# One share of dense tiles per pair of attention heads instead of two, in a two-layer transformer pair on one core

## The chip, the core and the metric

The kernel runs on one core of a Trainium2 chip. The metric is the device time of one execution in microseconds; the kernel before took 2789.5 us (median of 3 runs, 2788.83 to 2792.34). Of the core's engines the text names TensorE (PE, with PEld for its weight loads), VectorE (DVE), ScalarE (ACT), GpSimd (POOL) and SyncE (SP, which issues transfers).

## The reference

The input is a sequence of 512 rows of 1024 numbers, all in 32-bit floats. Two blocks of two layers each follow one another.

In a layer of the first block `h = x @ w_in` gives queries, keys and values of three attentions and three gates. The first ("fox") is causal softmax attention with a forgetting bias over 6 heads; the second is a stick-breaking attention over 5 heads; the third ("dsa") is softmax attention over 5 heads in which an index score picks at most 128 of the 512 keys per query. The outputs go through `w_up`, are multiplied with the sigmoids of the gates, summed, and projected by `w_out`; a layer norm and a feed-forward part follow.

In a layer of the second block a projection feeds a gated linear recurrence, a convolution branch and an attention ("nsa") of 8 heads with a compressed, a selected and a windowed branch. With 512 positions the selected and the windowed branch are both plain causal attention over all keys. The three results are concatenated and projected by `w_out`.

```
logits = q k^T * scale (+ bias);  w = softmax(mask(logits));  out = w v
merged = gate0 * (o_fox @ w_up_fox) + gate1 * (o_sb @ w_up_sb) + gate2 * (o_dsa @ w_up_dsa)
x = x + concat(y_nsa, y_lru, y_conv) @ w_out
```

## The kernel before, in words

Everything lies transposed (features on the partitions, 512 positions along the free axis). A dense product is cut into units of 8 tiles; a tile is one 128x128 piece of weights times 512 columns, and it takes three matmuls (`pe_tile`, L380 to L382), because weights and inputs are split into a high and a low part. The weights stream through four slots: SyncE loads `w_raw`, ScalarE rounds it to `w_hi` (L389), GpSimd makes `w_lo` (L404). When a unit is done, ScalarE takes its bank ("take", L1130 for the gates) and splits the weights of the slot's next unit.

Every engine has its own program, written out by hand; semaphores tie them. Nothing is reordered by a planner.

The softmax attentions fox, dsa and nsa share three functions, `pairs_pe`, `pairs_act` and `pairs_dve`. They run over "pairs": two heads (in dsa's last four pairs one head) at one block b of 128 queries, with (b + 1) * 128 keys; b runs 0, 1, 2, 3, 0, ... over the pairs n. A layer has 12 pairs in fox, 12 in dsa and 32 in nsa. For one pair:

- scores (TensorE, L494, and the mask L497) into the banks X[0] and X[1];
- the negated maximum (VectorE, L579);
- the exponential (ScalarE, L551) from these banks to the `work` tiles of the probabilities, with the row sums;
- the reciprocal and the scaling (VectorE, L587, L590 in nsa, L594), in place;
- the turn: transposes of the probabilities by TensorE (L507) into X[2] and ps[2];
- the copy of what was turned (ScalarE, L560);
- the values (TensorE, L521) into a bank that holds the output of two heads.

`depth` says how many buffers the probabilities and the turned copies have: 1 in fox, 2 in dsa and nsa. `exps(n)` waits for the turn of pair n - depth, and `copy(n)` for the values of pair n - depth. Scores of pair n wait until the exponentials of pair n - 1 have read the banks.

TensorE's order is in the loop of `pairs_pe`: scores of the next pair, `fill(n, 0)`, `turn(n)`, `fill(n, 1)`, `values(n - 1)`. Where scores need something of their own (`staged`: in fox at the first pair of each pair of heads, n + 1 = 4 and 8), they stand behind the turn. ScalarE's order is exps(n + 1), copy(n), and then takes and splits; in fox the takes stand in front of exps(n + 1), and a staging of the next queries and keys (`fox_stage`, L1172) follows copy(2) and copy(6). VectorE's is maximum(n + 1), scaling(n + 1), and then other work: in fox two rounds of a top-k search (L1317, L1319).

`fill` gives TensorE dense tiles that have nothing to do with the pair. In fox and dsa they are gate units (`gate_share`): `FOX_FILL` gives 3 units, 24 tiles, to each four pairs, so 3 tiles a call; `DSA_FILL` gives 2, 1 and 1 units, so 2, 1 and 1 tiles a call. In nsa they are tiles of the last projection (`out_fill`), one a call. ScalarE computes with `gate_ends` in which call a unit ends, and takes it one pair later (`round_gates`).

Of the kernel before, what the change touches and what calls it, by code (L numbers as in the profile page):

```python
# [28 lines left out]
QB = SEQ // P  # L29
# [28 lines left out]
FOX_FILL = ((4, 3), (7, 3), (10, 3))  # L58
STK_FILL = ((13, 3), (16, 2), (18, 2))
DSA_FILL = ((20, 2), (22, 1), (23, 1))  # L60
# [413 lines left out]
def half(e):  # L474
    return slice(64 * e, 64 * e + 64)


def count_before(pairs, n, e=0):

    return sum(len(h.heads) for h in pairs[:n]) + sum(x < e for x in pairs[n].heads)  # L480


def pairs_pe(S, pe, Z, h0, p0, pairs, ident, fill, ready, depth=2):
    nc = S.nc

    def scores(n):

        h = pairs[n]
        pe.wait_ge(Z.p, h0 + count_before(pairs, n))
        for sem, count in ready(n, "scores"):  # L490
            pe.wait_ge(sem, count)
        for e in h.heads:
            q, k = h.key(e)
            nc.tensor.matmul(S.X[e][:, 0:h.w], q, k, start=True, stop=False, skip_group_check=True)  # L494
        m, c = h.mask
        for e in h.heads:
            nc.tensor.matmul(S.X[e][:, c:h.w], S.idb[:, :], m, start=False, stop=True, skip_group_check=True).then_inc(Z.s, 1)  # L497

    def turn(n):
        h = pairs[n]  # L500
        pe.wait_ge(Z.ptc, h0 + count_before(pairs, n))
        for sem, count in ready(n, "turn"):
            pe.wait_ge(sem, count)
        for e in h.heads:
            pe.wait_ge(Z.scaled, h0 + count_before(pairs, n, e) + 1)
            for k in range(h.b + 1):
                m = nc.tensor.transpose((S.X[2], S.ps[2])[e][:, k * P:(k + 1) * P], h.probs[e][:, k * P:(k + 1) * P], ident)  # L507
            m.then_inc(Z.pt, 1)

    def values(n):  # L510
        h = pairs[n]
        pe.wait_ge(Z.ptc, h0 + count_before(pairs, n) + len(h.heads))
        for sem, count in ready(n, "values"):
            pe.wait_ge(sem, count)
        terms = [h.first] if h.first else []
        for k in range(h.b + 1):
            terms.append(lambda e, k=k: (h.value(e, k), h.turned[e][:, k * P:(k + 1) * P]))
        for x, term in enumerate(terms):
            for e in h.heads:
                v, p = term(e)  # L520
                m = nc.tensor.matmul(h.bank[half(e), h.b * P:h.w], v, p, start=(h.begins and x == 0),  # L521
                                     stop=(h.ends and x == len(terms) - 1), skip_group_check=True)
        m.then_inc(Z.o, 1)

    N = len(pairs)
    scores(0)
    for n in range(N):
        staged = n + 1 < N and any(True for _ in ready(n + 1, "scores"))
        if n + 1 < N and not staged:
            scores(n + 1)  # L530
        fill(n, 0)
        turn(n)
        if staged:
            scores(n + 1)
        fill(n, 1)
        if n >= 1:
            values(n - 1)
    values(N - 1)
# [66 lines left out]
def fox_pairs(S):  # L605

    pairs = []
    for n in range(3 * QB):
        i, b = divmod(n, QB)
        w = (b + 1) * P  # L610
        pairs.append(Pair(S, n, b, lambda e, b=b, w=w: (S.wk[e][:, b * P:w], S.wk[2 + e][:, 0:w]), (S.causb[:, :], b * P),
                          lambda e, k, i=i: vt_head(S, k, V_FOX, 2 * i + e), (S.ps[3], S.X[3])[i % 2], depth=1))
    return pairs
# [15 lines left out]
def dsa_pairs(S):  # L629

    pairs = []
    keys = [tile_rows(S, u, e) for e, u in ((0, A_DKIK), (1, A_S4KDK))]
    for n in range(3 * QB):
        i, b = divmod(n, QB)
        w = (b + 1) * P
        m0 = (b * (b + 1) // 2 - 1) * P
        q = [tile_rows(S, A_DQ + i if i < 2 else A_S4D4Q, e) for e in range(2)]
        pairs.append(Pair(S, n, b, lambda e, b=b, w=w, q=q: (q[e][:, b * P:w], keys[e][:, 0:w]),
                          (S.dmask[:, m0:m0 + w], 0) if b else (S.chunkb[:, :], 0),
                          lambda e, k: vt_head(S, k, V_DSA, 0), (S.ps[3], S.X[3])[i % 2], (0, 1) if i < 2 else (1,)))  # L640
    return pairs
# [302 lines left out]
def gate_fill(S, pe, L, i, first, tiles):  # L944


    for x in tiles:
        j, k = divmod(x, KT)
        u = A_GATE + first + j
        s = u % SLOTS  # L950
        if k == 0:
            pe.wait_ge(S.lo_ready[s], GA(L, u, i) + 1)
            pe.wait_ge(S.bank_free[(u - 2) % SLOTS], GA(L, u - 2, i) + 2)
        pe_tile(S, s, k, S.ps[u % 2][:, :], S.xh, S.xl, k, k == 0, k == KT - 1)
        if k == KT - 1:
            S.last.then_inc(S.unit_done[s], 1)


def gate_share(S, pe, L, fill, c, calls):

    first, units = fill
    n = units * KT
    gate_fill(S, pe, L, 0, first, range(n * c // calls, n * (c + 1) // calls))


def gate_ends(fill, calls):

    n = fill[1] * KT
    return [next(c for c in range(calls) if n * (c + 1) // calls >= KT * (j + 1)) for j in range(fill[1])]
# [5 lines left out]
def a_tensor(S, pe):  # L975
    nc = S.nc
    ident = S.con[:, C_ID:C_ID + P]
    for L in range(DEPTH):
# [11 lines left out]
        for v in range(A_NVT):  # L990
            if v >= 2:
                pe.wait_ge(S.vt_done, L * A_NVT + v - 1)
            for t in range(QB):
                m = nc.tensor.transpose(S.X[2 + v % 2][:, t * P:(t + 1) * P],
                                        S.qkv[:, A_VT[v] * SEQ + t * P:A_VT[v] * SEQ + (t + 1) * P], ident)
# [24 lines left out]
        def fox_ready(n, what):  # L1020
# [3 lines left out]
            if what == "values" and n == 2 * QB:  # L1024
                return [(S.fox.out, L * 3 + 1)]
            return []

        pairs_pe(S, pe, S.fox, L * 24, L * 12, fox_pairs(S), ident,
                 lambda n, x: gate_share(S, pe, L, FOX_FILL[n // QB], 2 * (n % QB) + x, 8), fox_ready)

        pe.wait_ge(S.fox.out, L * 3 + 2)
        for i in range(2):
# [7 lines left out]
        def dsa_ready(n, what):  # L1040
# [4 lines left out]
            if what == "values" and n == 2 * QB:  # L1045
                return [(S.dsa.out, L * 3 + 1)]
            return []

        pe.wait_ge(S.mask_ready, L + 1)
        pairs_pe(S, pe, S.dsa, L * 20, L * 12, dsa_pairs(S), ident,  # L1050
                 lambda n, x: gate_share(S, pe, L, DSA_FILL[n // QB], 2 * (n % QB) + x, 8), dsa_ready)

        for i in range(2):
            for jj in range(4):
# [15 lines left out]
                for w, x, stop in ((S.wh, S.rh, False), (S.wh, S.rl, False), (S.wl, S.rh, True)):  # L1070
                    for e, out in enumerate((XS, XD)):
                        m = nc.tensor.matmul(out, w[s][half(e), 5 * P:6 * P], x[half(e), 5 * SEQ:6 * SEQ], start=False, stop=stop)
# [50 lines left out]
def a_scalar(S, act, T):  # L1123
# [12 lines left out]
    for L in range(DEPTH):  # L1136
# [19 lines left out]
        def gate_take(j):  # L1156
            u = A_GATE + j
            take(u, G(u), cols(S.gates, j), ACT.Copy, 2)

        def gate_takes(fill, calls, c):  # L1160

            for j, end in enumerate(gate_ends(fill, calls)):
                if end == c:
                    gate_take(fill[0] + j)
# [21 lines left out]
        def round_gates(fill, n):  # L1186

            if n == 0:
                return
            i, m = divmod(n - 1, QB)  # L1190
            for x in range(2):
                gate_takes(fill[i], 2 * QB, 2 * m + x)

        def fox_after(n):
            if n % QB == 2 and n < 2 * QB:
# [25 lines left out]
        with act.Fori(0, 2) as i:  # L1221
            for jj in range(4):
                for d in range(3):
                    t = cols(S.gates, i * SLOTS + d * KT + jj)
                    m = nc.scalar.activation(t, t, ACT.Tanh, scale=0.5)
# [312 lines left out]
def GB(L, u, i=0):  # L1538

    return DEPTH * A_GROUPS + L * B_GROUPS + u // SLOTS + i  # L1540


def BF(L, u, i=0):

    s = u % SLOTS
    mine = [v for v in B_BANKED if v % SLOTS == s]
    return 1 + DEPTH * A_GROUPS + L * len(mine) + sum(v < u for v in mine) + i


def seq(t, j):  # L1550
    return t[:, j * SEQ:(j + 1) * SEQ]
# [73 lines left out]
def out_fill(S, pe, L, i, n):  # L1625


    j, k = divmod(n, KT)
    o, kk = divmod(k, 4)
    g = GB(L, B_OUTL, i)  # L1630
    if n == 0:
        if i == 0:
            pe.wait_ge(S.lru_done, L + 1)
        else:
            pe.wait_ge(S.mc_ready, L * 4 + 5)
    if k == 0:
        pe.wait_ge(S.lo_ready[j], g + 1)
        pe.wait_ge(S.first_added, L * 8 + i * 4 + j + 1)
    if k == 4:
        pe.wait_ge(S.bank_free[(j - 1) % SLOTS], BF(L, B_OUTL + j - 1, i) + 1 if j else BF(L, B_OUTL + 3, i))  # L1640
    pe_tile(S, j, k, S.ps[o][:, :], S.xh, S.xl, i * 4 + kk, kk == 0, kk == 3)
    if k == 3:
        S.last.then_inc(S.first_out, 1)
    if k == KT - 1:
        S.last.then_inc(S.unit_done[j], 1)
# [20 lines left out]
def b_tensor(S, pe):  # L1666
# [4 lines left out]
    for L in range(DEPTH):  # L1671
# [64 lines left out]
        for t in range(4):  # L1736
            m = nc.tensor.matmul(S.ps[1][:, :], S.ones[:, :], seq(S.cacc, t), start=(t == 0), stop=(t == 3))
# [24 lines left out]
        for q in range(4):  # L1762
            if q == 2:
                for t in range(4):
                    pe.wait_ge(S.cl_sq, L * 4 + t + 1)
                    m = nc.tensor.matmul(S.X[1][:, :], S.ones[:, :], S.lnsq[t][:, :], start=(t == 0), stop=(t == 3))
# [57 lines left out]
        def nsa_ready(n, what):  # L1824
# [3 lines left out]
            if what == "values" and n % (2 * QB) == 0 and n >= 4 * QB:  # L1828
                return [(S.mn_y, L * 4 + n // (2 * QB) - 1)]
            return []  # L1830

        pairs_pe(S, pe, S.nsa, L * 64, L * 32, nsa_pairs(S), ident,
                 lambda n, x: out_fill(S, pe, L, n // 16, n % 16 * 2 + x), nsa_ready)

        pe.wait_ge(S.first_added, L * 8 + 9)
        for j in range(4):
# [470 lines left out]
def program(nc, T, out):  # L2307
    with ExitStack() as ctx:
# [17 lines left out]
        @block.tensor  # L2326
        def _(pe):
            a_tensor(S, pe)
            b_tensor(S, pe)
# [174 lines left out]
```

## Time and profile before

| | |
|---|---|
| median of 3 runs | 2789.5 us |
| profiled execution | 2787.53 us, its span 2785.7 us |
| TensorE busy | 2693.0 us (97%) |
| VectorE, ScalarE, GpSimd busy | 1432.0, 1143.5, 1062.1 us |
| fox of the first layer, scores to last values | about 213 to 301 us into the span |
| dsa of the first layer | about 396 to 446 us |
| nsa of the two layers | about 2211 to 2339 and 2619 to 2747 us |

A line of the timeline gives the start of a group of equal instructions in us from the start of the span, the time from there to the end of the last, the engine and line, what it writes and reads, and how many there are. In brackets stand the idle time of the engine before it and what ended it. A record of a short matmul lasts 0.27 us though the next one starts after 0.11, because matmuls are pipelined.

### The profile page before, as it was taken

The numbers are of one execution on the slowest core, as the hardware profiler recorded it, in microseconds if no ns is written. First come the engines' busy times: TensorE is split into PE (matmuls) and PEld (weight loads), VectorE is DVE, ScalarE is ACT, GpSimd is POOL, SyncE is SP. The second block draws the span as 40 slices with busy tenths as digits, with TensorE's granted clock in tenths as the row PEclk, the third lists the DMA queues.
The fourth block names the chain that finished last, engine by engine and source line by source line (L and its number), as shares of the span: only waits on it lengthen the run. The fifth ranks groups of instructions, "written<-read, shape, count | busy, mean of one in ns | idle before, by whom it ended". The sixth has DMA issues, their size and how long they took to land.

```text
span 2785.7 us, 36067 instructions
## 1 busy us (share of the span) xinstructions
PE 2693.0 (97%) x12740; PEld 2046.6 (73%) x12740; DVE 1432.0 (51%) x2446; ACT 1143.5 (41%) x1982; POOL 1062.1 (38%) x430
## 2 busy tenths in 40 slices
PE   8999999999999989999999999999999999999998
PEld 6866666788888778576666888886687767787766
DVE  2067646562223220776474633232688764688764
ACT  2334435252223342444452522233436654337554
POOL 4422212344444434222123444443247522347612
PEclk9999999999999999999999999999999999999999
DMA  4221111222332223111122322322223211223211
GB/s 166 90 68 46 53 38 61 83 83 91 104 98 98 83 68 105 54 54 46 38 68 76 100 97 98 98 90 83 68 96 114 85 39 54 78 96 121 76 39 54
DMA packets 61316, 220.24 MB, mean 79 GB/s; under 512 B 6928, under 2 KB 7056, under 8 KB 61200
## 3 DMA queue, kind: packets, MB, share of 16 engines
q1 hardware_dynamic: 60624, 217.12, 23.8%
q8 instruction: 73, 1.20, 0.2%
q10 hardware_dynamic: 576, 1.57, 0.2%
q14 instruction: 43, 0.35, 0.0%
HBM read 216.57 MB, written 2.10 MB: 78 GB/s over the span
## 4 chain that ended last, share of the span: by engine, by line
PE 89%; DVE 5%; ACT 2%; DVEq 1%; POOL 1%; issue 1%; DMA 0%; ACTq 0%; SPq 0%
PE bank L380 24%; PE bank L382 24%; PE bank L381 24%; PE bank L494 3%; PE bank L521 3%; PE bank L507 2%; PE bank L843 1%; PE bank L709 1%; PE bank L497 1%; POOL w_lo L404 1%; PE bank L1014 1%; PE bank L731 1%; PE bank L727 1%; PE bank L701 1%; DVE proj L1376 1%
## 5 line engine op out<-in xcount | busy, mean ns | idle before, releaser
L404 POOL TENSOR_TENSOR w_lo<-w_raw,w_hi 128x1024 fp32r<-128x1024 f32 x404 | 1011.5, 2512 | 1694.1 <-ACT w_hi L389 1687.8
L380 PE MATMUL bank<-x_hi,w_hi 128*128 128x512 f32 x2128 | 883.0, 415 | 30.4 <-DVE x_lo L2301 11.0
L382 PE MATMUL bank<-x_hi,w_lo 128*128 128x512 f32 x2128 | 837.0, 393 | 0.0
L381 PE MATMUL bank<-x_lo,w_hi 128*128 128x512 f32 x2128 | 836.7, 393 | 0.0
L389 ACT ACTIVATE w_hi<-w_raw 128x1024 fp32r<-128x1024 f32 x400 | 419.6, 1055 | 435.1 <-PE bank L382 376.4
L380 PEld LDWEIGHTS bank<-x_hi,w_hi 128*128 128x128 f32 x2128 | 404.1, 190 | 149.9 <-issue 51.7
L382 PEld LDWEIGHTS bank<-x_hi,w_lo 128*128 128x128 f32 x2128 | 403.5, 190 | 87.4
L381 PEld LDWEIGHTS bank<-x_lo,w_hi 128*128 128x128 f32 x2128 | 404.7, 190 | 81.6 <-issue 9.6
L380 PE MATMUL bank<-rhs_hi,w_hi 128*128 128x512 f32 x624 | 245.4, 393 | 6.4 <-DVE rhs_lo L1449 6.4
L381 PE MATMUL bank<-rhs_lo,w_hi 128*128 128x512 f32 x624 | 243.5, 390 | 0.0
L382 PE MATMUL bank<-rhs_hi,w_lo 128*128 128x512 f32 x624 | 243.2, 390 | 0.0
L551 ACT ACTIVATE work<-bank,neg_max 128x128 f32<-128x128 f32 (+3 forms) x216 | 112.0, 523 | 213.8 <-DVE neg_max L579 162.4
L1514 DVE TENSOR_TENSOR ffn_sum<-ffn_sum,bank 128x512 f32 x64 | 43.9, 688 | 286.1 <-PE bank L382 286.1
L2071 DVE SCALAR_TENSOR_TENSOR bank<-glu_out,params_b_cur,bank 128x512 f32<-128x512 f32 x216 | 152.7, 752 | 34.2 <-issue 34.2
L1504 DVE TENSOR_TENSOR work<-work 128x512 f32<-128x512 f32 x64 | 90.8, 1419 | 139.1 <-ACT rhs_hi L1271 139.1
L1361 DVE TENSOR_SCALAR proj<-proj 128x1024 f32<-128x1024 f32 (+2 forms) x8 | 9.3, 1227 | 267.7 <-ACT proj L1130 267.7
L380 PEld LDWEIGHTS bank<-rhs_hi,w_hi 128*128 128x128 f32 x624 | 117.5, 188 | 36.3 <-issue 11.7
L382 PEld LDWEIGHTS bank<-rhs_hi,w_lo 128*128 128x128 f32 x624 | 117.5, 188 | 24.7
L381 PEld LDWEIGHTS bank<-rhs_lo,w_hi 128*128 128x128 f32 x624 | 117.6, 188 | 23.8
L579 DVE TENSOR_REDUCE neg_max<-bank 128x1 f32<-128x128 f32 (+3 forms) x216 | 96.1, 485 | 65.7 <-PE bank L497 64.2
L1269 ACT ACTIVATE work<-bank 128x512 f32<-128x512 f32 x64 | 38.0, 594 | 193.2 <-PE bank L382 185.0
L1130 ACT ACTIVATE proj<-bank 128x512 f32 (+1 forms) x52 | 31.0, 596 | 201.5 <-PE bank L382 201.5
(390 smaller groups left out, 3327.5 us busy)
## 6 DMA issues: line engine op xcount, KB each, us to landing
w_raw<-w SPq DMA_DIRECT2D x404, 512.0 KB, 3.4
ln_in<-x SPq DMA_DIRECT2D x4, 512.0 KB, 7.7
out<-residual SPq DMA_DIRECT2D x8, 256.0 KB, 2.2
p_raw<-p ACTq DMA_DIRECT2D x2, 512.0 KB, 4.1
constants<-con SPq DMA_DIRECT2D x1, 455.0 KB, 10.4
cos<-cos SPq DMA_DIRECT2D x1, 256.0 KB, 10.5
sin<-sin SPq DMA_DIRECT2D x1, 256.0 KB, 10.2
params_b<-prm_b ACTq DMA_DIRECT2D x1, 256.0 KB, 3.1
```

Source lines behind the costliest of these rows:

```text
L380: nc.tensor.matmul(out, wh, xh, start=first, stop=False)
L381: nc.tensor.matmul(out, wh, xl, start=False, stop=False)
L382: S.last = nc.tensor.matmul(out, wl, xh, start=False, stop=last)
L389: S.nc.scalar.activation(S.wh[s][:, :], S.raw[s][:, :], ACT.Copy).then_inc(S.hi_ready[s], 1)
L404: S.nc.gpsimd.tensor_tensor(S.wl[s][:, :], S.raw[s][:, :], S.wh[s][:, :].bitcast(F32), ALU.subtract).then_inc(S.lo_ready[s], 1)
L494: nc.tensor.matmul(S.X[e][:, 0:h.w], q, k, start=True, stop=False, skip_group_check=True)
L507: m = nc.tensor.transpose((S.X[2], S.ps[2])[e][:, k * P:(k + 1) * P], h.probs[e][:, k * P:(k + 1) * P], ident)
L521: m = nc.tensor.matmul(h.bank[half(e), h.b * P:h.w], v, p, start=(h.begins and x == 0), stop=(h.ends and x == len(terms) - 1), skip_group_ ...
L551: nc.scalar.activation(h.probs[e][:, 0:h.w], S.X[e][:, 0:h.w], ACT.Exp, bias=S.nm[x][:, :], accum_out=S.rs2[:, x:x + 1]).then_inc(Z.p, 1)
L579: nc.vector.tensor_reduce(S.nm[2 * h.par + e][:, :], S.X[e][:, 0:h.w], AX, ALU.max, negate=True).then_inc(Z.max, 1)
L1504: nc.vector.tensor_tensor(h, S.wk[j % 2][:, :], S.wk[j % 2][:, :], ALU.mult)
L2071: stt(out=S.X[t % 2][:, :], in0=S.uc[:, bass.ds(i * 3 + (k + t * UC_W), SEQ)], scalar=S.curB[:, bass.ds(i * 3 + (k + PB_DW + t * CONV_K), ...
```

## The change

`fill` is called once per pair, ahead of the turn, and gives what the two calls gave together. In fox and dsa it asks for one of 4 shares in place of two of 8; in nsa it issues the two tiles one behind the other. ScalarE's list of takes is computed for 4 calls.

```diff
@@ pairs_pe
         if n + 1 < N and not staged:
             scores(n + 1)
-        fill(n, 0)
+        fill(n)
         turn(n)
         if staged:
             scores(n + 1)
-        fill(n, 1)
         if n >= 1:
             values(n - 1)
@@ a_tensor (fox; dsa alike, with DSA_FILL)
-                 lambda n, x: gate_share(S, pe, L, FOX_FILL[n // QB], 2 * (n % QB) + x, 8), fox_ready)
+                 lambda n: gate_share(S, pe, L, FOX_FILL[n // QB], n % QB, QB), fox_ready)
@@ a_scalar, round_gates
-            for x in range(2):
-                gate_takes(fill[i], 2 * QB, 2 * m + x)
+            gate_takes(fill[i], QB, m)
@@ b_tensor (nsa)
-                 lambda n, x: out_fill(S, pe, L, n // 16, n % 16 * 2 + x), nsa_ready)
+                 lambda n: [out_fill(S, pe, L, n // 16, n % 16 * 2 + x) for x in range(2)], nsa_ready)
```

## Rows read from the trace of the kernel before

**Rows 1.** The page, busy us (share of the span) and instructions.

```profile
PE 2693.0 (97%) x12740; PEld 2046.6 (73%) x12740; DVE 1432.0 (51%) x2446; ACT 1143.5 (41%) x1982; POOL 1062.1 (38%) x430
```

**Rows 2.** The waits of TensorE: total us, times, longest.

```profile
PE bank L494 <- ACT work L551: 9.6, 6, 2.2
...
PE bank L507 <- DVE work L594: 4.0, 6, 0.8
```

**Rows 3.** Timeline, fox of layer 1, turn of pair 5 to scores of pair 7.

```profile
254.75 0.60 PE L507 MATMUL bank<-constants,work 128*128 128x128 f32 x4
255.11 0.48 PE L380 MATMUL bank<-x_hi,w_hi 128*128 128x512 f32 x1
...
257.36 0.44 PE L521 MATMUL bank<-work,v_tok 128*64 128x128 f32 x4
257.73 1.98 PE L494 MATMUL bank<-work,work 128*128 128x512 f32 x4
...
255.45 0.58 ACT L551 ACTIVATE work<-bank,neg_max 128x384 f32<-128x384 f32 x1 [3.72 <-PE bank L507]
...
256.48 0.20 ACT L551 ACTIVATION_READ_ACCUMULATOR work<-bank,neg_max 128x1 f32 x1
```

**Rows 4.** Timeline, fox of layer 1, exponentials of pair 5 and values of pair 3.

```profile
248.72 0.48 ACT L551 ACTIVATE work<-bank,neg_max 128x256 f32<-128x256 f32 x1 [1.53 <-DVE neg_max L579]
...
249.54 0.20 ACT L551 ACTIVATION_READ_ACCUMULATOR work<-bank,neg_max 128x1 f32 x1
...
250.08 1.09 PE L521 MATMUL bank<-work,v_tok 128*64 128x128 f32 x16
```

**Rows 5.** Timeline, fox of layer 1, around the staged scores of pair 4.

```profile
236.23 0.20 ACT L551 ACTIVATION_READ_ACCUMULATOR work<-bank,neg_max 128x1 f32 x1
...
238.42 2.32 ACT L1172 ACTIVATE work<-proj 64x512 f32<-64x512 f32 x4
...
239.67 1.04 PE L507 MATMUL bank<-constants,work 128*128 128x128 f32 x8
240.84 0.68 PE L494 MATMUL bank<-work,work 128*128 128x128 f32 x4
...
241.98 0.49 DVE L579 TENSOR_REDUCE neg_max<-bank 128x1 f32<-128x128 f32 x2
...
242.30 0.37 ACT L551 ACTIVATE work<-bank,neg_max 128x128 f32<-128x128 f32 x1
...
242.91 0.20 ACT L551 ACTIVATION_READ_ACCUMULATOR work<-bank,neg_max 128x1 f32 x1
...
243.68 0.88 PE L521 MATMUL bank<-work,v_tok 128*64 128x128 f32 x12
```

**Rows 6.** Timeline, end of dsa of layer 1 and start of the products behind it.

```profile
443.80 0.60 ACT L560 ACTIVATE work<-bank 128x512 f32<-128x512 f32 x1 [1.75 <-PE bank L507]
...
444.50 0.60 ACT L1130 ACTIVATE gates<-bank 128x512 f32<-128x512 f32 x1
...
449.17 0.77 PE L380 MATMUL bank<-rhs_hi,w_hi 128*128 128x512 f32 x1 [3.04 <-DVE rhs_lo L1449]
```

**Rows 7.** Timeline, nsa of layer 1: its start, and a later pair.

```profile
2217.53 0.66 PE L507 MATMUL bank<-constants,work 128*128 128x128 f32 x2 [0.82 <-DVE work L594]
...
2218.43 0.20 ACT L551 ACTIVATION_READ_ACCUMULATOR work<-bank,neg_max 128x1 f32 x1
...
2219.41 1.23 PE L494 MATMUL bank<-b_ks,b_q 64*128 64x256 f32 x4
...
2259.88 0.58 ACT L551 ACTIVATE work<-bank,neg_max 128x384 f32<-128x384 f32 x1 [2.28 <-DVE neg_max L579]
...
2260.92 0.20 ACT L551 ACTIVATION_READ_ACCUMULATOR work<-bank,neg_max 128x1 f32 x1
...
2261.53 0.92 PE L494 MATMUL bank<-b_kw,b_q 64*128 64x384 f32 x4
```

**Rows 8.** Stretch of dsa: its length, busy us by engine, PEclk, DMA.

```profile
395.00:446.00 51.00, 49.83 (x311) 33.69 (x309) 20.27 (x55) 24.32 (x69) 9.41 (x4) 1.00 0.13 42
```

More of the change, by code:

```diff
@@ L1050, in a_tensor @@
         pairs_pe(S, pe, S.dsa, L * 20, L * 12, dsa_pairs(S), ident,
-                 lambda n, x: gate_share(S, pe, L, DSA_FILL[n // QB], 2 * (n % QB) + x, 8), dsa_ready)
+                 lambda n: gate_share(S, pe, L, DSA_FILL[n // QB], n % QB, QB), dsa_ready)
         for i in range(2):
```

## The prediction, made before the change was run

> **What bounds the kernel now.** I read the busy table first: TensorE works 2693 of 2785.7 us [rows 1]. The profiled execution took 2787.53 us, so 1.8 us lie around its span, and the median of the runs shown, 2789.5, is 2.0 above it. TensorE is the bound nearly everywhere, so the change can gain only what TensorE waits for in the three attentions, or what it pays for going from one kind of matmul to another. The waits of TensorE come next: its scores waited 9.6 us in all for exponentials and its turns 4.0 us for the scaled probabilities [rows 2]. Those 4.0 us are the whole stock of waits that a later turn can remove. Then I read the timelines of the stages, TensorE beside ScalarE, for who ends each wait and how much room there is where none is seen.
>
> Names: pair n has scores S(n), exponentials E(n), turns T(n), copies C(n) and values V(n). fox is the first attention, dsa the second, nsa the third; they have 12, 12 and 32 pairs in each of two layers, 112 in all. A share is 9 dense matmuls in fox, 6 or 3 in dsa, 3 in nsa.
>
> **What moves.** Before, TensorE runs S(n+1), share, T(n), share, V(n-1), S(n+2). After, it runs S(n+1), both shares, T(n), V(n-1), S(n+2). No matmul is added or dropped. ScalarE's takes of finished gate units stay at the same pairs, since with 24, 16 or 8 tiles the last tile of a unit falls in the same pair for 8 calls as for 4; no DMA is issued elsewhere. Nor does V(n-1) get a new wait: it needs C(n-1), for which T(n) has waited already. What is late next is S(n+2). It needs E(n+1), because scores write over the banks that the exponentials read. In dsa and nsa E(n+1) needs only its own maximum and a much older turn (depth 2). In fox (depth 1) it writes over the probabilities that T(n) reads, so E(n+1) starts when T(n) is over. Between T(n) and S(n+2) there were a share and V(n-1), now V(n-1) alone.
>
> **Transitions.** Per pair the path from the last transpose to V was 255.08 to 257.36, 2.28 us [rows 3]: 255.08 is the group's start 255.11 minus 0.03, or 254.75 plus three steps of 0.11. Of it 9 matmuls at 0.229 are 2.06, which are merely moved. What remains, 0.22, is to be set against the new step from a transpose straight to V. From V to S the same rows give it: the last V starts at 257.53 (start plus 0.44 minus the last one's 0.27), S at 257.73, 0.20 later, that is one 128-column pass (0.11) and 0.10 of emptying. I take 0.21, since T to V changes the shape of the array's use (128x128 to 128x64) as V to S does. Gain 0.01 x 112, nothing. Bounds: 0.03, as a dense matmul's record stands behind the last transpose [rows 3], and 0.40, as S stands behind T at the start of a head pair [rows 5]; that is -0.19 to +0.18 each, -21 to +20 us over 112 pairs.
>
> The trace's 0.10 agrees with a rule of the Trainium skill (TensorEngine Tiling, "Key Properties"): a change of tiling mode, as opposed to tile, drains the engine. By it T to V costs a drain just as share to V did, so this item is nothing; without it the item would be -11 us (112 x 0.10).
>
> **fox, the cost.** In the trace T(5) starts its last transpose at 255.08 and E(6) starts at 255.45, released by the turn: 0.37 later. E(6) is over at 256.68 and S(7) comes at 257.73 [rows 3]: 1.05 of room, which a share of 2.06 had made. From E's end to a waiting S I take 0.05 (an estimate: nothing lies between but the signal, and if it is 0.2 the sum grows by 2). E takes 1.02 for 256 columns [rows 4] and 1.23 for 384 [rows 3], so 0.21 a step, 0.81 for 128 [rows 5] and 1.44 for 512. From V to S is V's record less 0.27 plus the 0.20: 0.37 for one block (257.36 to 257.73), 0.81 for three [rows 5], 1.02 for four [rows 4], 0.59 for two by the same steps. After the change S(n+2) stands ready at 0.21 + V(n-1) behind the last transpose, and its banks at 0.42 + E(n+1). The new wait is the difference, 0.21 + E(n+1) - V(n-1):
> - S(3), S(7), S(11): E of 384, V of one block: 0.21 + 1.23 - 0.37 = 1.07 each, 3.2 together.
> - S(6), S(10): E of 256, V of four blocks: 0.21 + 1.02 - 1.02 = 0.2 each, 0.4. In the trace E(5) was released by VectorE's maximum [rows 4]; with the turn 2.06 later it is the turn.
> - S(2): no values yet, and scores may follow a transpose at 0.11: 0.42 + 1.02 - 0.11 = 1.3.
> - S(4), S(8) are issued behind T(3), T(7) (staged), so S(5), S(9) come close behind them. Set the last transpose of T(2) to 0. E(3) ends at 0.37 + 1.44 = 1.81. In the trace VectorE reduces S(4) at 241.98, 5.55 after E(3)'s end 236.43, with its top-k rounds before [rows 5]; after: 7.36. E(4) starts 0.32 later and takes 0.81, so S(5) may go at 8.54. TensorE: V(1) at 0.21, 0.59 long, 18 matmuls 4.21 (18 x 0.229 and 0.09 at their start), T(3) to its last transpose 0.77, then 0.11: S(4) at 5.9. S lasts 0.68 - 0.27 + 0.11 = 0.52 [rows 5], mask to V 0.21 (two of 0.055 and the 0.10), V(2) 0.81, ready at 7.4. Wait 1.1. Against it S(4) loses a wait of 0.29: it started 0.40 behind the last transpose (239.67 + 0.77), because ScalarE's staging ended at 240.74 [rows 5]. Net 0.8 each, 1.6.
> - S(1), V(11): as before; the latter waits for a copy that starts behind V(10).
>
> Sum 3.2 + 0.4 + 1.3 + 1.6 = 6.5 a layer, 13.1 for two. Nothing later gives it back, as TensorE is the bound behind it.
>
> **dsa.** The periods between scores stay, and E doesn't wait for the turn. But the last turn T(11) is 0.69 later (3 x 0.229), and C(11) started on it, with ScalarE idle 1.75 before. Behind C(11) on ScalarE are the take of the last gate unit, a split and the rounding of the outputs, and for those TensorE waits 3.04 [rows 6]. The take started at 444.50; it will follow C(11), which starts at 443.80 + 0.69 and lasts 0.60: 445.09 at the latest, +0.59. I take +0.5 a layer, as records of neighbours overlap a little, +1.0. Bounds: 0 if the delay is hidden, 1.4 with the full 0.69.
>
> **nsa.** In steady state nothing: S(n+2) follows S(n+1) at the same distance and the least room in front of it, 0.41, hangs on maxima and not on turns [rows 7]. Copies are up to 0.69 later, but ScalarE idled longer than that before E, 2.28 at that pair [rows 7]. At the start T(0) waited 0.8 for scaled probabilities [rows 7, 2]; the second share now lies in that wait. S(2) stood at 2219.41 and is then held by E(1), over at 2218.63, so 2218.68: -0.7 a layer, -1.4. The other waits of this kind (1.2 us at pair 5) are refunded to nobody, since E(6) holds S(7) there; lower end -4.0 for all of rows 2.
>
> **Sum.** 13.1 + 1.0 - 1.4 + 0 = +12.7 us on the profiled 2787.5: 2800.2; on the median of 2789.5, 2802. That is 0.45%.
>
> **Rivals.**
> 1. The turn hands over to the values for less than I say. At 0.11 (no emptying) the item is -11 and the time 2791, no change; at 0.03 it is -20, and the time 2782, faster. It decides against me from 0.10 less a pair. For it: the record of a dense matmul 0.03 behind a transpose. Against: the 0.20 from V to S, and that the dense record behind the transpose lasts 0.48, so that its start is no start of streaming. 7% for no change, 4% for faster.
> 2. VectorE becomes fox's bound. Its top-k rounds fill most of the 5.55 us quoted above, and E(4) had no slack. If some four maxima a layer come late by 1.2 each: +9.6, 2812. For it: VectorE's 5.55 against a pair of 7.3 us (V(3) at 250.08, V(4) at 257.36, [rows 3, 4]). Against: the turn that releases E is later too. 7%.
> 3. The waits drop TensorE's clock in fox. Each new gap is 1.3 at most, and the dsa stage has TensorE idle for 1.17 us (51.00 less 49.83), nearly all of it in one wait before S(1), at a granted clock of 1.00 [rows 8]. At half the clock the 216 matmuls of fox's shares alone would take 0.2 more each, +43 a layer. 2%: over 2830.
> 4. fox does not pay: exponentials are early enough by some path that I overlooked. The room of 1.05 against the 2.06 that is removed speaks against it, as does the releaser in the row. The time is then 2789. 4%.
>
> **Numbers.** Mine 76%, rival 1 11%, rival 2 7%, rival 3 2%, rival 4 4%. What a measurement tells from no change is about 0.2%, 5.6 us: faster 0.05, same 0.11, slower 0.84. Range 2793 to 2812: down by half of my fox waits and a part of rival 1, up to rival 2 or a T to V of 0.29.
>
> **What would show it.** In fox of the changed kernel: a wait of S on E in the list of waits, six to eight times a layer, most near 1 us, about 14 us more than the 9.6 of now; E released by the turn at every pair; from the last transpose to V about 0.21. In dsa the wait of 3.04 becomes about 3.5. In nsa the first turn's wait is gone, S(2) is some 0.7 nearer to S(0), and the stage is otherwise as long as before. I am wrong if fox's stage is less than 3 us a layer longer, or if nsa gets shorter by more than 2.

## The result, and the profile after

| | median, us | runs | ratio to before, 95% interval |
|---|---|---|---|
| before | 2791.4 | 8 | |
| after | 2802.2 | 8 | 1.0042 [1.0029, 1.0054] |

The change makes the kernel slower by 0.42%, 8 to 15 us by the interval. The profiled execution of after took 2806.32 us (span 2804.5), 18.8 more than that of before. Not all of that comes from the changed code: the matmuls of code that is the same in both already differ in where the clock is low (below), and TensorE's wait for its first inputs, within the first 60 us, was 12.6 us here and 11.0 in before (10.8 to 13.3 over the profiles of all kernels). So the steps are judged on the stages alone, and the total on the medians.

The waits of TensorE, as in [rows 2] (lines from L532 on have moved by one or two):

```profile
PE bank L494 <- ACT work L550: 24.2, 22, 2.2
...
PE bank L380 <- DVE rhs_lo L1447: 6.8, 2, 3.4
```

Scores wait 24.2 us for exponentials where they waited 9.6 [rows 2]: 14.6 more, in 16 more places. Of these 12.8 are fox's, in six places a layer (2 x (1.17 + 3 x 1.01 + 2 x 1.10)); the other 1.8, in four places, are nsa's. The row of turns that wait for scaled probabilities (4.0) is gone.

The timeline of fox of layer 1 around T(5), which [rows 3] show before:

```profile
262.32 0.60 PE L507 MATMUL bank<-constants,work 128*128 128x128 f32 x4
262.84 0.44 PE L521 MATMUL bank<-work,v_tok 128*64 128x128 f32 x4
...
264.30 1.98 PE L494 MATMUL bank<-work,work 128*128 128x512 f32 x4 [1.01 <-ACT work L550]
...
263.01 0.58 ACT L550 ACTIVATE work<-bank,neg_max 128x384 f32<-128x384 f32 x1 [5.98 <-PE bank L507]
...
264.04 0.20 ACT L550 ACTIVATION_READ_ACCUMULATOR work<-bank,neg_max 128x1 f32 x1
```

These five lines show how the loss comes about. The exponentials start 0.36 behind the last transpose (262.32 + 3 x 0.11 = 262.65), as before; they are over at 264.24, 1.23 later. But now only V(4), four matmuls, stands between the turn and the next scores, and the scores wait. The 1.01 in brackets is the idle time behind the last record of V; scores can start 0.07 ahead of that record's end (the 0.27 of a record less the 0.20 from V to S), so the whole wait is 1.08. From the last transpose to V is 0.19.

Exponentials of 256 columns, which VectorE released before [rows 4], are now released by the turn, and the first ones of a head pair still by the maximum:

```profile
255.55 0.47 ACT L550 ACTIVATE work<-bank,neg_max 128x256 f32<-128x256 f32 x1 [3.38 <-PE bank L507]
...
249.82 1.13 PE L494 MATMUL bank<-work,work 128*128 128x256 f32 x4 [1.10 <-ACT work L550]
...
248.96 0.37 ACT L550 ACTIVATE work<-bank,neg_max 128x128 f32<-128x128 f32 x1 [1.35 <-DVE neg_max L578]
```

The end of dsa, as in [rows 6]:

```profile
452.82 0.60 ACT L559 ACTIVATE work<-bank 128x512 f32<-128x512 f32 x1 [2.11 <-PE bank L507]
...
453.31 0.59 ACT L1129 ACTIVATE gates<-bank 128x512 f32<-128x512 f32 x1
...
457.98 0.47 PE L380 MATMUL bank<-rhs_hi,w_hi 128*128 128x512 f32 x1 [3.42 <-DVE rhs_lo L1447]
```

The start of nsa, as in [rows 7]: the turn waits for nothing, and S(2) for E(1).

```profile
2237.91 0.63 PE L507 MATMUL bank<-constants,work 128*128 128x128 f32 x2
2238.80 1.22 PE L494 MATMUL bank<-b_ks,b_q 64*128 64x256 f32 x4 [0.26 <-ACT work L550]
```

The steps from one S to the next (start to start of L494 in the timeline, us) show which pair pays. fox, S(2) to S(3) and so on to S(11), layer 1; "idle" is that in front of the later one:

| | S3 | S4 | S5 | S6 | S7 | S8 | S9 | S10 | S11 | sum |
|---|---|---|---|---|---|---|---|---|---|---|
| before | 6.50 | 10.84 | 3.65 | 6.62 | 6.62 | 10.84 | 3.65 | 6.62 | 6.62 | 61.96 |
| after | 7.67 | 12.58 | 2.63 | 6.80 | 7.68 | 12.58 | 2.62 | 6.82 | 7.67 | 67.05 |
| idle, after | 1.01 | 0 | 1.10 | 0.15 | 1.01 | 0 | 1.10 | 0.15 | 1.01 | 5.5 |

From S(2) to S(11) it is 5.09 more; layer 2 agrees (67.02 against 61.96). In front of S(2) TensorE is idle for 1.17, and 0.16 more are lost to the record's length (0.27 less the 0.11 after which scores may follow a transpose): 1.33. fox costs 6.4 a layer, 12.8 in all.

The step S(1) to S(2) itself grew by 2.72, from 7.09 to 9.81. Of that 1.33 are the ones just named; the other 1.4 are not the change. Behind the 2.2 us for which TensorE waits before S(1), in both kernels, its granted clock is at the half level (1.2 of 2.4 GHz) for a while: dense matmuls last 0.63 and come every 0.43, then 0.39 and every 0.23. The mean granted clock was 0.67 from 217.00 to 226.90 in after, and 0.76 from 216.50 to 223.50 in before. How long the half level lasts differs from execution to execution of the same instructions (table below, "S1 to S2"), with this change and without it; the same holds at the start of nsa.

### The profile page after: what moved, and what is told of

Read it like the earlier page. It is cut to its first block, busy times and chain, and to the rows that moved or that the text cites. A ratio compares the mean times of both kernels' runs of the same rounds, so it can differ in the third digit from the quotient of the medians.

```text
span 2804.5 us, 36067 instructions
## 1 busy us (share of the span) xinstructions
PE 2698.7 (96%) x12740; PEld 2063.5 (74%) x12740; DVE 1429.5 (51%) x2446; ACT 1145.5 (41%) x1982; POOL 1061.1 (38%) x430
## 4 chain that ended last, share of the span: by engine, by line
PE 88%; DVE 6%; ACT 3%; DVEq 1%; issue 1%; POOL 1%; DMA 0%; ACTq 0%; SPq 0%
PE bank L380 24%; PE bank L381 23%; PE bank L382 23%; PE bank L494 3%; PE bank L521 3%; PE bank L507 2%; PE bank L842 1%; PE bank L1013 1%; ACT work L550 1%; PE bank L708 1%; POOL w_lo L404 1%; PE bank L497 1%; PE bank L730 1%; PE bank L726 1%; PE bank L700 1%
## 5 line engine op out<-in xcount | busy, mean ns | idle before, releaser
L404 POOL TENSOR_TENSOR w_lo<-w_raw,w_hi 128x1024 fp32r<-128x1024 f32 x404 | 1010.5, 2510 | 1713.9 <-ACT w_hi L389 1707.3
L380 PE MATMUL bank<-x_hi,w_hi 128*128 128x512 f32 x2128 | 875.1, 411 | 31.5 <-DVE x_lo L2299 12.6
L380 PEld LDWEIGHTS bank<-rhs_hi,w_hi 128*128 128x128 f32 x624 | 117.8, 189 | 37.1 <-issue 12.4
```

The source lines that it names most:

```text
L380: nc.tensor.matmul(out, wh, xh, start=first, stop=False)
L404: S.nc.gpsimd.tensor_tensor(S.wl[s][:, :], S.raw[s][:, :], S.wh[s][:, :].bitcast(F32), ALU.subtract).then_inc(S.lo_ready[s], 1)
```

## The experiments

Kernels of one table stand beside runs of the kernel before on their chip. `tail` is dense work that `pairs_pe` issues behind the turn and behind staged scores, and `fox_tiles(n, a, b)` issues the tiles from a up to b, b left out, of the six of pair n:

```diff
 def pairs_pe(..., fill, ready, tail=lambda n: None):
         if staged:
             scores(n + 1)
+        tail(n)
         if n >= 1:
             values(n - 1)
```

| kernel | fox, tiles ahead + behind the turn | dsa, nsa: shares | median, us (before) | ratio, 95% interval | S2 to S11, us | S1 to S2, both layers | TensorE's scores on exponentials |
|---|---|---|---|---|---|---|---|
| after | 6 + 0 | 1, 1 | 2802.2 (2791.4) | 1.0042 [1.0029, 1.0054] | 67.05 | 9.81, 9.55 | 24.2 |
| fox alone | 6 + 0 | 2, 2 | 2801.0 (2790.6) | 1.0037 [1.0024, 1.0051] | 67.04 | 9.80, 8.45 | 22.4 |
| fox apart | 3 + 3 | 1, 1 | 2788.6 (2790.6) | 0.9992 [0.9981, 1.0003] | 61.96 | 8.41, 8.10 | 12.0 |
| second buffers | 6 + 0 | 1, 1 | 2788.3 (2790.6) | 0.9990 [0.9980, 0.9999] | 61.69 | 8.10, 8.11 | 13.2 |
| 5 and 1 | 5 + 1 | 1, 1 | 2791.4 (2790.6) | 1.0000 [0.9991, 1.0009] | 63.21 | 8.64, 7.72 | 15.7 |
| 4 and 2 | 4 + 2 | 1, 1 | 2787.1 (2791.6) | 0.9983 [0.9974, 0.9992] | 61.28 | 7.10, 8.12 | 11.8 |
| 0 and 6 | 0 + 6 | 1, 1 | 2801.9 (2791.6) | 1.0043 [1.0030, 1.0056] | 67.53 | 7.08, 6.99 | 12.0 |
| no top-k | 6 + 0 | 1, 1 | 2800.7, one run | | 65.56 | 8.39, 8.39 | 21.9 |
| nsa's first pair | 6 + 0 | 1, 1 at pair 0 | 2802.7, one run | | 67.06 | 6.82, 9.71 | 23.4 |
| the gains | 4 + 2 | 2, 1 | 2787.4 (2790.6) | 0.9983 [0.9975, 0.9992] | 61.30 | 8.39, 7.13 | 11.8 |
| before, second buffers | 3 + 3 | 2, 2 | 2790.3 (2790.6) | 0.9996 [0.9988, 1.0005] | 61.95 | 8.48, 8.21 | 9.6 |

S2 to S11 is layer 1's, from the start of S(2) to that of S(11); before it is 61.96, and S1 to S2 is 7.09 and 7.13. The last column, in us over both layers, holds 4.4 us in front of S(1) of fox in every kernel; the rest of before's 9.6 are 2.3 in front of S(1) of dsa and 2.8 in nsa.

**Fox alone, and fox apart.** One edit on after each:

```diff
@@ fox alone: dsa with two shares again (nsa alike, with out_fill)
-                 lambda n: gate_share(S, pe, L, DSA_FILL[n // QB], n % QB, QB), dsa_ready)
+                 lambda n: gate_share(S, pe, L, DSA_FILL[n // QB], 2 * (n % QB), 8), dsa_ready,
+                 lambda n: gate_share(S, pe, L, DSA_FILL[n // QB], 2 * (n % QB) + 1, 8))
@@ fox apart: fox with 3 tiles ahead of the turn and 3 behind it
-                 lambda n: gate_share(S, pe, L, FOX_FILL[n // QB], n % QB, QB), fox_ready)
+                 lambda n: fox_tiles(n, 0, 3), fox_ready, lambda n: fox_tiles(n, 3, 6))
```

> fox has one share per pair, dsa and nsa have two as before. My theory (the loss is fox's exponentials, which are released by the turn): fox costs what it costs in the changed kernel, +15 us on the profiled execution of before (13 by the forecast, 15 by the stage in the changed kernel's trace), a ratio of 1.0047 to 1.0055; waits of scores on exponentials 24 us, 22 times, as in the changed kernel. Rival 'every pair pays, in all three attentions' (the step from a turn to values): 112 pairs share the loss, 24 of them are here, so fox alone costs 3 us, ratio 1.001. Where mine holds, this kernel is 1 to 2 us slower than the changed kernel, because nsa's gain of 2.7 and dsa's loss of 0.5 are left out.

> dsa and nsa have one share per pair, fox has two again (3 tiles ahead of the turn, 3 behind it). My theory: the whole loss is fox's, so this is 2 us faster than before (nsa -2.7, dsa +0.5 or +1 in its end), ratio 0.9992, no wait of scores on exponentials beyond the 9.6 us of before. Rival 'every pair pays': 88 of 112 pairs still have one share, so 0.8 of the loss stays, ratio 1.003.

Fox alone shows all of the loss (1.0037; 112 pairs sharing it would have given 1.001), and fox apart none of it. The loss is fox's. My ratio for fox alone, 1.0047 to 1.0055, was too high: its upper part came from the 15 us of the profiled stage, part of which is the clock's, and the 12.8 of the steps are 1.0046, inside the measured interval. I had also expected it to be 1 to 2 us slower than after, as it lacks nsa's gain; the medians (2801.0 and 2802.2) don't resolve that. Its scores wait 22.4 us in 18 places, not 24 in 22, as the four places of nsa are gone. The waits on exponentials in fox apart are 12.0, not the 9.6 that I expected: in nsa scores now wait a little where the turn did before. That is no extra time, since the same kernel's turns lost 2.7 of their 4.0.

**Second buffers** for fox's probabilities, place and number of the shares as in after (odd pairs get two tiles of their own; shortened):

```diff
@@ Pair of fox
+                          probs=(otok(S, 6), otok(S, 7)) if n % 2 else None))
@@ pairs_act, exps
-            if n >= depth:
-                act.wait_ge(Z.pt, h0 + count_before(pairs, n - depth) + len(pairs[n - depth].heads))
+            if n >= 2:
+                act.wait_ge(Z.pt, h0 + count_before(pairs, n - 2) + len(pairs[n - 2].heads))
```

> The changed kernel with a second pair of buffers for fox's probabilities (two tiles of the outputs' buffer that are free in that stage): exponentials of pair n+1 now need the turn of pair n-1 and not of n. The turned copy keeps one buffer. Nothing else differs; order and place of the shares are those of the changed kernel. My theory: the waits before S(2), S(3), S(6), S(7), S(10), S(11) go, because exponentials start on their maximum, some 2 us sooner. S(5) and S(9) keep about 0.7 (the maximum of the staged S(4) and the exponentials of 128 columns, 2.3 us, against mask and V(2), 1.5 us behind its start). fox is then within 1 us a layer of before, total between -2 and +1 against before, ratio 0.9993 to 1.0003. Rival VectorE (its two top-k rounds a pair set when maxima and scalings come): a second buffer does not hasten VectorE, most of the 14.6 us of waits stay, now released by the maximum, ratio 1.004. Rival 'merged shares themselves cost' (more steps between kinds of matmul or the clock): ratio 1.004 with no waits in the list.

The waits of fox that are left behind S(1), in layer 1, are these two:

```profile
246.09 1.13 PE L495 MATMUL bank<-work,work 128*128 128x256 f32 x4 [0.36 <-ACT work L551]
...
273.70 1.13 PE L495 MATMUL bank<-work,work 128*128 128x256 f32 x4 [0.36 <-ACT work L551]
```

The six others are gone, fox is as short as before (61.69 against 61.96), and with it the loss: 0.9990, a little below the 0.9993 to 1.0003 that I expected. So what cost time was that E(n+1) must follow T(n), which rests on one buffer, and not the shares as such. VectorE's part in it is measured below. S(5) and S(9) kept 0.36, half of the 0.7 I expected: from the start of S(4) to the end of its exponentials is 1.83 (244.21 to 246.04), where I had put 2.3.

**Before with second buffers** is the control: the same two edits on the kernel before.

> The kernel before with the second pair of buffers for fox's probabilities, as a control for the kernel that has them and one share. Theory: with a share of 2.06 us behind the turn no score waits for exponentials, so earlier exponentials are worth nothing: ratio 0.9995 to 1.0005, steps S to S of fox from S(2) on equal to before within 0.1 but for S(4) and S(8), which wait 0.13 for the staging. Rival: the second buffers are a gain of their own (ScalarE or VectorE ahead), ratio 0.998, and the level time of the kernel with one share and second buffers was two effects that cancel.

0.9996: alone they are worth nothing, as their exponentials were early already. What they gave above is the cure of the change's own wait.

**5 and 1, 4 and 2** tiles: `fox_tiles(n, 0, 5)` and `(n, 5, 6)`, or 4 in place of 5.

> The changed kernel, in fox 5 of a pair's 6 tiles ahead of the turn and 1 behind it (behind staged scores too). One tile is 0.69 us. My theory, by the subtraction it rests on: the wait is 1.07 - 0.69 = 0.4 before S(3), S(7), S(11); nothing before S(6), S(10); 1.1 - 0.69 = 0.4 before S(5), S(9); 1.2 - 0.69 = 0.5 before S(2). Together 2.5 a layer where the changed kernel has 7.3, so 9.6 us fewer waits in two layers, and fox is some 5 us (2 layers) longer than before: about +3 on before with nsa's and dsa's parts, ratio 1.001. Rival VectorE: waits before S(5), S(9) stay 1.1. Rival T to V: the step from a turn to values is gone, for it is a dense tile again, so all of the loss goes at once: as the kernel with 3 and 3 tiles.

> The changed kernel, in fox 4 of a pair's 6 tiles ahead of the turn and 2 (1.37 us) behind it. Theory (a wait is what is left of 0.21 + E - V after the dense tiles between turn and scores): 1.37 is more than the largest wait of the changed kernel, 1.17, so every wait of scores on exponentials behind S(1) is gone; fox from S(2) on is as long as with 3 and 3 tiles; total 2 us under before, ratio 0.9992, the same as 3 and 3 within the measurement. Rival 'the loss grows with each tile that is moved': a third of it stays, ratio 1.001.

The waits of 5 and 1 (timeline, layer 1; S(2), S(3), S(5), and S(7), S(9) repeat the last two):

```profile
224.17 1.56 PE L494 MATMUL bank<-work,work 128*128 128x384 f32 x4 [0.47 <-ACT work L551]
231.16 1.98 PE L494 MATMUL bank<-work,work 128*128 128x512 f32 x4 [0.31 <-ACT work L551]
...
245.70 1.13 PE L494 MATMUL bank<-work,work 128*128 128x256 f32 x4 [0.39 <-ACT work L551]
```

One tile behind the turn takes 0.70 off each of 1.17, 1.01 and 1.10, and three matmuls at 0.229 are 0.69. fox is then 1.9 longer a layer than before, where I had put 2.5, and the time is level with before (1.0000, expected 1.001). With two tiles behind it no wait is left but the one before S(1), as I expected. I had also expected fox to be level with before, and it is 0.68 a layer shorter (61.28 against 61.96, in both layers). The fourth tile ahead of T(3) and T(7) gives the staging 0.69 more time, and S(4) and S(8), which stood 0.40 behind the last transpose [rows 5], now follow it 0.11 later (241.02 to 241.13 in its timeline): two of 0.29, most of the 0.68. So a wait is a plain difference of two paths, the third tile behind the turn buys nothing, and ahead of it it buys something.

**0 and 6**: one share, all behind the turn (`fox_tiles(n, 0, 0)` and `(n, 0, 6)`).

> The changed kernel, in fox all 6 tiles of a pair behind the turn: one share per pair, as in the changed kernel, but in the other place. Theory (place and not number of the shares sets the loss): no wait of scores on exponentials; a turn now follows the scores directly and could wait for its scaled probabilities, but the exponentials start 4 us sooner, so it does not, but for T(0), within 1.5 us a layer. fox within 1.5 us a layer of 3 and 3 tiles, ratio 0.9990 to 1.0003. Rival 'one share of six tiles costs, wherever it stands': ratio 1.004. Rival 'the turn waits instead' (scaled probabilities late at every pair by 0.5 or more): 12 us over both layers, ratio 1.004, with the waits put down to the scaling.

My theory failed here: 1.0043, as slow as after, by other waits. The rival that one share costs wherever it stands gave this ratio too, but second buffers have one share and no loss, and the waits say what it was. In front of T(3) and S(4) (layer 1; TensorE, then ScalarE):

```profile
236.16 0.66 PE L521 MATMUL bank<-work,v_tok 128*64 128x128 f32 x8
237.84 1.09 PE L507 MATMUL bank<-constants,work 128*128 128x128 f32 x8 [1.03 <-ACT work L560]
240.09 1.19 PE L494 MATMUL bank<-work,work 128*128 128x128 f32 x4 [1.15 <-issue]
```

```profile
236.92 0.87 ACT L560 ACTIVATE work<-bank 128x384 f32<-128x384 f32 x2 [3.26 <-PE bank L521]
237.68 2.31 ACT L1175 ACTIVATE work<-proj 64x512 f32<-64x512 f32 x4
```

With one buffer of turned probabilities C(2) needs V(1), and T(3) needs C(2), which empties its banks. A share used to lie between V(1) and T(3). Where the scores are staged nothing is between them now: T(3) waits 1.03 for the copy, and S(4) 1.15, by its place for the staging that stands behind the copy on ScalarE (it ends at 239.99, and S(4) starts at 240.09; the row itself names no releaser). T(7), S(8) and T(11) do the same: 5.4 a layer. Behind the two waits in front of S(4) the granted clock falls to the half level as well, in both layers, but not at S(8), where they are as long:

```profile
232.00:240.00 8.00, 5.91 (x36) 4.42 (x34) 5.95 (x16) 4.51 (x11) 2.10 (x1) 0.99 0.18 66
240.00:243.20 3.20, 3.11 (x11) 2.69 (x12) 1.02 (x4) 2.33 (x6) 1.57 (x1) 0.50 0.00 0
243.20:260.00 16.80, 16.73 (x97) 12.82 (x95) 12.82 (x33) 5.11 (x14) 3.20 (x2) 1.00 0.19 63
```

(Stretch, its length, busy us of PE, PEld, DVE, ACT, POOL, granted clock, DMA.) The half clock costs 1.5 there: S(4) to S(5) is 7.21, S(8) to S(9) 5.71. So the rule "behind the turn is safe" would be as false as "ahead of it": each place has a buffer of depth 1 behind it, the probabilities the one and the turned copy the other, and the share has to be cut so that both are covered.

**No top-k**, for VectorE's part. It leaves out the two rounds in each pair of fox, and so computes another result; it is one run, and only its waits are read:

```diff
@@ fox_after
-            for x in range(2):
-                top_round(S, dve, x)
```

> The changed kernel without the two top-k rounds that VectorE has in each pair of fox (24 of 32 selection rounds are left out; the key selection of the third attention is another one). It asks what part VectorE has in the waits. Theory: only S(5) and S(9) wait for VectorE: in the changed kernel its rounds hold the maximum of S(4) until 1.44 us behind the scores' start (247.19 to 248.64), in the kernel with double buffers it comes at 0.70. So these two waits fall from 1.10 to 0.36, and those before S(2), S(3), S(6), S(7), S(10), S(11) stay at 1.17, 1.01, 0.15, 1.01, 0.15, 1.01. Waits of fox fall from 6.7 to 5.2 a layer. Rival VectorE (it bounds fox): all waits fall below 0.4.

```profile
250.35 1.13 PE L494 MATMUL bank<-work,work 128*128 128x256 f32 x4 [0.36 <-ACT work L550]
...
264.83 1.98 PE L494 MATMUL bank<-work,work 128*128 128x512 f32 x4 [1.01 <-ACT work L550]
```

S(5) (and S(9)) went from 1.10 to 0.36, and the rest stayed at 1.17, 1.02, 0.15, 1.01, 0.15, 1.01. VectorE holds 0.74 in two places a layer, 3 us in all. In after one sees it hold the maximum of S(4), whose last product starts at 247.52 (247.19 plus three steps of 0.11):

```profile
247.88 0.68 DVE L1317 MATCH_REPLACE8 idx_score<-top,idx_score 128x512 f32<-128x512 f32 x1
248.63 0.49 DVE L578 TENSOR_REDUCE neg_max<-bank 128x1 f32<-128x128 f32 x2
```

**Nsa's first pair**: one share at pair 0, two at all others; one run, read for its steps.

```diff
-                 lambda n: [out_fill(S, pe, L, n // 16, n % 16 * 2 + x) for x in range(2)], nsa_ready)
+                 lambda n: [out_fill(S, pe, L, n // 16, n % 16 * 2 + x) for x in range(1 if n else 2)], nsa_ready,
+                 lambda n: n and out_fill(S, pe, L, n // 16, n % 16 * 2 + 1))
```

> The changed kernel, in nsa only the first pair with both tiles ahead of the turn, all others with one ahead and one behind as before. It asks which pair gives nsa's gain. Theory: the step S(1) to S(2) stays 5.03 (0.7 under before), for the second tile fills the wait of T(0); the step S(5) to S(6) goes back from 4.44 to 5.34, because the tile ahead of T(4) and what stands behind it on ScalarE and GpSimd are again where they were. Steady steps 0.01 longer each. Rival: the step of pair 5 depends on the start alone (GpSimd's products shifted against VectorE), and stays 4.44.

S(1) to S(2) stayed at 5.01, S(5) to S(6) went back to 5.34, and steady steps are 0.01 longer, as expected. So nsa's gain has two places: 0.7 comes from the share of pair 0, and 0.9, in front of S(6), from the shares of the pairs behind it; the turn that had waited there is that of pair 4.

**The gains** alone: fox 4 and 2, dsa two shares, nsa one.

> The parts of the change that gain, without those that lose: nsa with both tiles ahead of the turn, dsa with two shares, fox with 4 tiles ahead of the turn and 2 behind it. Theory: nsa gives 1.6 a layer (0.7 before S(2), 0.9 before S(6)) less nothing, fox is level with before from S(2) on, dsa too, with the wait in front of the products behind it back at 3.04: 3 us under before, ratio 0.9989. It differs from the kernel with 4 and 2 tiles in fox by dsa's second share alone, 0.5 a layer at most, so the two can't be told apart by time. Rival: the gain of nsa is given back later (a wait of the products behind it grows by as much), ratio 1.0000.

0.9983, and the wait in front of the products behind dsa is back at 3.0 (6.4 in two layers, against 6.8). By its steps it gains 5 us and not the 3 that I expected, since fox of 4 and 2 tiles is not level but 1.4 shorter over both layers; the times don't tell the two apart (0.9989 lies inside the interval). This and the kernel with 4 and 2 tiles beat both before and after; their two medians, 2787.4 and 2787.1, are alike.

## Why the prediction was right

I forecast +12.7 us, 2802; the median is 2802.2. By step:

- **Transitions** (nothing, bounds -21 to +20): right. T to V takes 0.19 where I took 0.21. In nsa the 25 steps from S(6) to S(31) are 0.15 shorter together, in dsa S(2) to S(11) 0.1 of 37.1, so that is a gain of 0.01 a pair. The drain that the Trainium skill (TensorEngine Tiling, "Key Properties") names for a change of mode is paid on either path: 0.19 from T to V and 0.20 from V to S, where one pass is 0.11.
- **fox, S(3), S(7), S(11)**: 1.07 forecast, 1.08 measured. **S(6), S(10)**: 0.2 and 0.22 (0.15 of idle time and the 0.07). **S(2)**: 1.3 and 1.33. **S(5), S(9)**: 1.1 and 1.17, of which the refund at S(4), S(8) leaves 0.72 for both steps together (0.8 forecast). Sum 6.5 forecast, 6.4 measured. The mechanism was tried from three sides: more dense work between turn and scores shortens each wait by its own length, a second buffer removes them, undoing fox removes the loss.
- **dsa**: +0.5 a layer forecast for the wait in front of the products. The wait grew by 0.38 (3.04 to 3.42), and the way from S(11) to the products by 0.47 (10.49 to 10.96); the steps give back 0.1. That is +0.4 a layer, 0.7 in all.
- **nsa**: -0.7 a layer at S(2), measured -0.74 (5.77 to 5.03). Wrong was the next sentence: the waits of turns behind it (1.2 us) "are refunded to nobody". They are those of T(4), not of pair 5 as I wrote, and the scores behind them are S(6), which E(5) holds. S(5) to S(6) is 0.90 shorter, in both layers. I had looked only at whether E holds the next scores, and it does, for 0.59 us. But E came sooner, since its maximum did. The size of the error is 1.8 us of 2790, below what the times can tell; the trace shows it. With it nsa is 1.8 shorter a layer, 3.6 in all, where -1.4 in all was forecast: taken over both layers, my own sign of being wrong ("shorter by more than 2") came up for this stage.
- **Rivals.** The cheap step from turn to values is out by the 0.19, and by fox apart, whose 88 merged pairs are no slower and no faster than the parts of nsa and dsa explain (-2.9 us by the steps, 0.9990; 0.9992 measured). VectorE as fox's bound is out: its part is 0.74 at S(5) and S(9), which stood in the forecast. The clock stayed at 1.00 in fox of after behind its start (226.90 to 302.00, and in layer 2 1209 to 1290); but 0 and 6 shows that the rival was nearer than the 2% I gave it: behind waits of 1.03 and 1.15 with 1.1 of work between them the clock fell at S(4) and not at S(8). That fox does not pay at all is out by the 24.2 us of waits and by fox alone.

Adding up what was measured: fox 12.8, dsa 0.7, nsa -3.6 (0.74, 0.90 and 0.15 a layer), together +9.9, inside the interval of +8 to +15. The forecast's +12.7 is inside it too; its excess over the sum of the stages is for the most part nsa's. That the median fell on the forecast to 0.2 us is luck: the times don't tell 9.9 from 12.7. The same sums give 1.0046 for fox alone, 0.9988 for second buffers, 1.0003 for 5 and 1, 0.9985 for 4 and 2, and 0.9982 for the gains, each inside its measured interval.

## What to carry to other kernels

Before moving filler work, write down for each buffer of depth 1 the loop it closes (turn, exponentials, next scores; or values, copy, next turn) and how much filler lies inside it: the wait that appears is the loop's length less the filler and the other work left inside it, here to about 0.1 us. Filler that covers a loop is worth nothing beyond its length (here two tiles of six), so the rest may stand wherever another wait can use it. Where there is room for a second buffer, it can take the filler's part: here it removed six of eight waits a layer with all six tiles ahead of the turn, and left 0.36 at the other two.

## What the runs showed of the hardware

**Some VectorE instructions stand still while GpSimd's runs.** In nsa of before, at the scaling of pair 4, GpSimd's product (L442) starts just ahead of a VectorE product of 128x2 elements, and that lasts 1.28 us, where it lasts 0.16 in later pairs:

```profile
2229.34 5.21 POOL L442 TENSOR_TENSOR x_lo<-silu_z_conv,x_hi 128x512 fp32r<-128x512 f32 x4
2229.36 1.28 DVE L590 TENSOR_TENSOR gate_inv<-gate_inv,b_gate_tok 128x2 f32<-128x2 f32 x1
...
2230.71 2.70 DVE L594 TENSOR_SCALAR work<-work,gate_inv 128x384 f32<-128x384 f32 x2
```

In after VectorE's product starts 0.33 ahead of GpSimd's L442. It is held only by what is left of GpSimd's weight product (L404, over at 2249.45), ends 0.02 behind that one after 0.39, and has not to wait for L442:

```profile
2247.06 2.39 POOL L404 TENSOR_TENSOR w_lo<-w_raw,w_hi 128x1024 fp32r<-128x1024 f32 x1 [4.58 <-ACT w_hi L389]
...
2248.84 0.17 DVE L586 RECIPROCAL gate_inv<-row_sums 128x2 f32<-128x2 f32 x1 [0.84 <-ACT work L550]
2249.08 0.39 DVE L589 TENSOR_TENSOR gate_inv<-gate_inv,b_gate_tok 128x2 f32<-128x2 f32 x1
...
2249.41 5.21 POOL L442 TENSOR_TENSOR x_lo<-silu_z_conv,x_hi 128x512 fp32r<-128x512 f32 x4
2249.55 2.72 DVE L593 TENSOR_SCALAR work<-work,gate_inv 128x384 f32<-128x384 f32 x2
```

The maximum behind them, that of S(5), comes at 2252.19, 2.6 behind the start of S(5), and no longer 3.4; that is the 0.90 that I missed. With one share at pair 0 and two at pairs 1 to 4, the kernel with nsa's first pair has the slow order again (GpSimd at 2246.43, the product at 2246.45 for 1.27).

The Trainium skill (SBUF — State Buffer, "SBUF: two separate sides") says that the ports which VectorE and GpSimd share are held for its whole length by whichever instruction came first, a GpSimd one or a VectorE one of certain kinds: in a mode that uses both ports, or with two inputs in SBUF against a GpSimd one that reads SBUF. The traces agree: the product of 2 columns, with two inputs in SBUF, ends 0.02 behind GpSimd's instruction in both kernels, and the reciprocal, with one input, lasts 0.17 beside L404 as it does alone. The scalings of 384 columns last 1.35 each beside GpSimd's 1.3, against 0.42 alone; which kind they are no run here tells.

**The half clock lasts differently in the same code.** After the 2.2 us wait in front of S(1), S(1) to S(2) took 7.09 and 7.13 in before and 8.41 and 8.10 in fox apart, whose instructions there are the same. In after, fox alone and nsa's first pair, also the same as one another there and with the 1.33 of S(2) in it, it took 6.82 to 9.81. That is up to 3 us of difference between executions at one place, a quarter of this change. The Trainium skill (TensorE: Matmul & The Clock Gate, "What's actually happening") says of the slow matmuls at the start of a kernel that their number varies from run to run of the same kernel; these rows agree, and show it in the middle of one. Why nearly the same pair of waits dropped the clock at S(4) and not at S(8) of the kernel with 0 and 6 tiles stays open.
